# A hybrid decoder trunk on one core: the delta-rule mixer in single steps between half projection units

## The reference

```python
w = -softplus(-(decay_w0 + tanh(wl) @ decay_w2)) - 0.5
decay = exp(-exp(w));  a = sigmoid(aaa_a0 + al @ aaa_w2);  g = sigmoid(gl) @ gate_w2
kk = k * k_k;  kk = kk / max(norm(kk), 1e-12)          # per head of 64
k = k * (1 + (a - 1) * k_a)
# per token, state S (64x64) per head, 8 heads:
S = S * decay + (S @ -kk) (kk * a)^T + v k^T;   y = S @ r
y = groupnorm(y) * gn_g + gn_b + (r * k * r_k).sum() * v;   out = y * g
```

## Time and profile before

| | |
|---|---|
| Median of 3 runs | 1887.74 us (1887.35 to 1894.12) |
| The profiled execution | 1885.17 us, span 1883.4 us |
| Busy: PE, PEld, DVE, ACT, POOL | 1731.8, 1532.1, 1368.5, 1002.6, 31.1 us |
| Mean granted PE clock | 0.969 |
| Read from HBM | 408.09 MB, 218 GB/s over the span |

### The profile page before, as it was taken

One profiled execution on the slowest core, in us unless ns is written; L12 is line 12 of the kernel. 1 busy time (PEld: TensorE's weight loads), 2 busy tenths in 40 slices (PEclk: granted clock), 3 DMA queues, 4 the chain that ended last, 5 costly groups with the idle time before them and its releaser, 6 DMA issues.

```text
span 1883.4 us, 27888 instructions
## 1 busy us (share of the span) xinstructions
PE 1731.8 (92%) x10784; PEld 1532.1 (81%) x10784; DVE 1368.5 (73%) x1242; ACT 1002.6 (53%) x919; POOL 31.1 (2%) x20
## 2 busy tenths in 40 slices
PE   6898998879999789899989599999999999999996
PEld 6797897868999679888888488888888888888885
DVE  5757755675444676766475688989898988888887
ACT  4363243633333344523344376767676776767674
POOL 0000000001000200000000100000000000000000
PEclk9899999998999799999999799999999999999998
DMA  8322322464665343223234598989999999999993
GB/s 262 114 91 90 112 86 91 136 179 134 178 178 178 122 147 112 90 88 93 68 121 168 190 351 321 374 318 379 330 374 331 356 337 360 331 362 354 342 364 121
DMA packets 252061, 411.29 MB, mean 218 GB/s; under 512 B 8400, under 2 KB 133840, under 8 KB 251344
## 3 DMA queue, kind: packets, MB, share of 16 engines
q1 hardware_dynamic: 249440, 400.68, 61.6%
q10 hardware_dynamic: 2544, 9.54, 1.4%
HBM read 408.09 MB, written 2.10 MB: 218 GB/s over the span
## 4 chain that ended last, share of the span: by engine, by line
PE 78%; DVE 14%; ACT 4%; issue 4%; DMA 1%; SPq 0%; DVEq 0%; ACTq 0%
PE W L428 16%; PE W L430 16%; PE W L429 16%; PE Y L428 5%; PE Y L429 5%; PE Y L430 5%; PE Y L596 2%; PE Y L590 2%; PE Y L785 2%; ACT w_hi L952 2%; DVE w_lo L1330 2%; PE W L505 1%; DVE sc L1475 1%; PE Y L505 1%; DVE xt L1492 1%
## 5 line engine op out<-in xcount | busy, mean ns | idle before, releaser
L428 PE MATMUL W<-w_lo,x_hi 128*128 128x512 f32 (+1 forms) x1120 | 393.0, 351 | 9.1 <-DVE x_lo L1629 6.5
L430 PE MATMUL W<-w_hi,x_hi 128*128 128x512 f32 (+1 forms) x1120 | 387.6, 346 | 0.0
L429 PE MATMUL W<-w_hi,x_lo 128*128 128x512 f32 (+1 forms) x1120 | 386.9, 345 | 0.0
L1330 DVE TENSOR_TENSOR w_lo<-raw,w_hi 128x2048 fp32r<-128x2048 f32 x115 | 263.2, 2292 | 165.7 <-ACT w_hi L952 164.6
L1337 DVE TENSOR_TENSOR w_lo<-raw,w_hi 128x2048 fp32r<-128x2048 f32 x144 | 329.7, 2290 | 52.5 <-ACT w_hi L958 52.3
L958 ACT ACTIVATE w_hi<-raw 128x2048 fp32r<-128x2048 f32 x144 | 276.0, 1917 | 83.3 <-PE Y L430 43.7
L428 PE MATMUL W<-x_lo,w_hi 128*128 128x256 f32 x992 | 294.2, 297 | 22.1 <-DVE w_lo L1330 15.7
L1337 DVE TENSOR_TENSOR w_lo<-raw_more,w_hi 128x2048 fp32r<-128x2048 f32 x120 | 275.0, 2291 | 32.0 <-ACT w_hi L958 31.9
L429 PE MATMUL W<-x_hi,w_lo 128*128 128x256 f32 x992 | 285.7, 288 | 0.0
L430 PE MATMUL W<-x_hi,w_hi 128*128 128x256 f32 x992 | 285.4, 288 | 0.0
L958 ACT ACTIVATE w_hi<-raw_more 128x2048 fp32r<-128x2048 f32 x120 | 230.7, 1922 | 67.1 <-PE W L430 43.9
(11 more groups left out here) (278 smaller groups left out, 2097.7 us busy)
## 6 DMA issues: line engine op xcount, KB each, us to landing
raw<-w_in SPq DMA_DIRECT2D x124, 512.0 KB, 4.7
raw<-moe_gate SPq DMA_DIRECT2D x48, 1024.0 KB, 7.0
raw<-moe_up SPq DMA_DIRECT2D x48, 1024.0 KB, 7.7
raw<-moe_down SPq DMA_DIRECT2D x48, 1024.0 KB, 6.2
raw_more<-moe_gate SPq DMA_DIRECT2D x40, 1024.0 KB, 7.5
raw_more<-moe_up SPq DMA_DIRECT2D x40, 1024.0 KB, 7.3
raw_more<-moe_down SPq DMA_DIRECT2D x40, 1024.0 KB, 6.9
raw<-w_branch SPq DMA_DIRECT2D x24, 512.0 KB, 4.4
```

Source lines behind the costliest of these rows:

```text
L428: nc.tensor.matmul(out_ap, lhs[0], rhs[1], start=start, stop=False)
L429: nc.tensor.matmul(out_ap, lhs[1], rhs[0], start=False, stop=False)
L430: return nc.tensor.matmul(out_ap, lhs[0], rhs[0], start=False, stop=stop)
L1330: V.tensor_tensor(w_lo[u % 3][:], raw[u % 3][:], w_hi[u % 3][:].bitcast(F32), ALU.subtract)\
```

## The change

1. Entries ("front", kind, q) and ("back", kind, q) take half a unit each: PE issues 24 matmuls, ACT and DVE do the splits of unit u+2 at the front, ACT copies the bank at the back. Nearly every step of the mixer stands between two halves.
2. Levels 1 to 5 of the inversion act only inside the two 64x64 blocks on a matrix's diagonal. They are kept compactly (128 partitions x 64): mc, ac, xn and xt[:, :, 0]. Each product is two 64x64 matmuls for each of 8 matrices. Both x and its transpose are updated by matmul and addition, so the transposes go. Level 6 is the corner block alone. The masks cm are cut to this form by POOL at the start.
3. The chain is split in cg, cu and cy; its copies move from DVE to ACT.
4. The sums for the two norms are taken by token (4 products with two columns), square root and reciprocal act on 8 numbers for each partition, and 8 matmuls spread them over the channels (spread, scaled).
5. The token shift becomes ACT's copy times mu, and one DVE operation. ksq, decayed, the copy of y and the squares move to ACT; gn_b is added to the bonus on ACT.
6. The last two units of gate1 move ahead of the end of the second inversion.

```diff
+    ("front", "rkv", 5), ("spread", 0), ("kk", 0), ("back", "rkv", 5), ("prep", 0),
+    ("units", "conv", 0, 1), ("decayed", 0), ("shift", 1),
+    ("front", "conv", 1), ("tok", 0), ("bonus", 0), ("back", "conv", 1), ("scores", 0, 0),
+    ("front", "conv", 2), ("scores", 0, 1), ("back", "conv", 2), ("compact", 0), ("lora_w", 1), ("rate_w", 1),
+    ("front", "conv", 3), ("invert", 0), ("back", "conv", 3), ("mx", 0, 1), ("shift", 3),
+    ("front", "conv", 4), ("dx", 0, 1), ("back", "conv", 4), ("mx", 0, 2), ("shift", 5),
+    ("front", "conv", 5), ("dx", 0, 2), ("back", "conv", 5), ("mx", 0, 3), ("decay", 1), ("lora_a", 1), ("rate_a", 1),
+    ("front", "gate0", 0), ("dx", 0, 3), ("back", "gate0", 0), ("mx", 0, 4), ("ksq", 1), ("exps", 1), ("conv", 0),
+    ("front", "gate0", 1), ("dx", 0, 4), ("back", "gate0", 1), ("mx", 0, 5), ("ss", 1), ("knorm", 1),
+    ("front", "gate0", 2), ("dx", 0, 5), ("back", "gate0", 2), ("mx", 0, 6), ("conv", 1), ("osplit", 0), ("spread", 1), ("kk", 1),
...
+    ("units", "qkv", 3, 4), ("compact", 1),
+    ("front", "qkv", 4), ("invert", 1), ("back", "qkv", 4), ("mx", 1, 1), ("rope", 2),
...
+    ("front", "gate1", 3), ("dx", 1, 5), ("back", "gate1", 3), ("mx", 1, 6), ("dx", 1, 6),
+    ("cg", 1, 0), ("cu", 1, 0), ("cy", 1, 0), ("cg", 1, 1), ("cu", 1, 1), ("cy", 1, 1), ("yrow", 1),
+    ("mean", 1), ("var", 1), ("scaled", 1), ("osplit", 1), ("heads",), ("units", "branch1", 0, 2),
...
+            def over_channels(to):
+                for c in range(NT):
+                    for m in range(2):
+                        for h, half in enumerate(HALVES):
+                            last = nc.tensor.matmul(tiles(to[:])[half, m, c * P:(c + 1) * P],
+                                                    inv[:, c, m, h:h + 1].to_broadcast([P, HD]), ident, start=True, stop=True)
...
+            def blocks(bank, left, right):
+                for u in range(8):
+                    for half in HALVES:
+                        last = nc.tensor.matmul(tiles(bank[:], 8)[half, u, :], left(half, u), right(half, u), start=True, stop=True)
...
+            def dx(l, p, v):            # PE
+                if v < TOP:
+                    blocks(Y[1], lambda half, u: mc[half, u, :], lambda half, u: xt[half, u, 0, :])
+                    last = blocks(Y[2], lambda half, u: xt[half, u, 0, :], lambda half, u: mc[half, u, :])
...
+            def front(l, kind, q):      # ACT
+                split_hi(layer_unit(l) + UNIT0[kind] + q + 2)
...
+            def compact(l, p):          # ACT
+                act.wait_ge(sem("score_ready"), 8 * n + 8)
+                for half in HALVES:
+                    last = A(ac[half], sc[half, :, 0, half], ACT.Copy)
...
+            def front(l, kind, q):      # DVE
+                u = layer_unit(l) + UNIT0[kind] + q
+                split_lo(u + 2)
...
+            def invert(l, p):           # DVE
+                dve.wait_ge(sem("ac_ready"), n + 1)
+                link(V.tensor_tensor(mc[:], ac[:], each_of_8(0), ALU.mult))
+                mark(V.tensor_tensor(xt[:, :, 0, :], mc[:], each_of_8(TOP), ALU.add), "xt0_ready", n + 1)
+                mask_level(n, 1)
...
+            def dx(l, p, v):            # DVE
+                V.tensor_tensor(xt[:, :, 0, :], xt[:, :, 0, :], tiles(Y[1][:], 8), ALU.add)
+                mark(V.tensor_tensor(xn[:], xn[:], tiles(Y[2][:], 8), ALU.add), "x_ready", 5 * n + v)
+                if v < TOP - 1:
+                    mask_level(n, v + 1)
```

More of the change, by code:

```diff
@@ L125 @@
     ("units", "rkv", 1, 2), ("shift", 0), ("lora_w", 0), ("rate_w", 0),
[L126 to L148, removed]
@@ L149 @@
-    ("units", "gate1", 1, 2), ("chain", 1, 0), ("chain", 1, 1), ("finish", 1),
-    ("units", "gate1", 2, 4), ("osplit", 1), ("heads",), ("units", "branch1", 0, 2),
+    ("units", "rkv", 2, 3), ("decay", 0), ("lora_a", 0), ("rate_a", 0),
+    ("spill",), ("units", "rkv", 3, 4), ("shift", 2), ("ksq", 0), ("exps", 0),
+    ("units", "rkv", 4, 5), ("ss", 0), ("knorm", 0), ("shift", 4),
+    ("front", "rkv", 5), ("spread", 0), ("kk", 0), ("back", "rkv", 5), ("prep", 0),
+    ("units", "conv", 0, 1), ("decayed", 0), ("shift", 1),
@@ L558, in scores @@
                 pe.wait_ge(sem("bonus_ready"), n + 1)
[L559 to L569, removed]
@@ L631, in chain @@
                     cols = slice(c * P, (c + 1) * P)
-                    pair = [(h, hc, half) for h, mm, hc, half in heads if mm == m]
+                    pair = [(h, hc, half) for h, mm, hc, half in HEADS if mm == m]
                     for h, hc, half in pair:
@@ L904, in _ @@
             handlers = {"units": units, "lora_w": lora_w, "lora_a": lora_a, "ss": ss, "tok": tok, "scores": scores, "invert": invert,
-                        "level": level, "chain": chain, "finish": finish, "rope": rope, "heads": heads, "att_scores": att_scores,
+                        "front": front, "back": back, "mx": mx, "dx": dx, "cg": cg, "cu": cu, "cy": cy, "spread": spread,
+                        "mean": mean, "var": var, "scaled": scaled, "rope": rope, "heads": heads, "att_scores": att_scores,
                         "probs_t": probs_t, "att_out": att_out}
@@ new lines, in ksq @@
+            def ksq(l, p):
+                n = 2 * l + p
+                act.wait_ge(sem("shifted"), 7 * l + order[2 + p] + 1)
+                if n:
+                    act.wait_ge(sem("score_done"), 8 * n)
+                    act.wait_ge(sem("bonus_done"), n)
+                for m in range(2):
+                    last = A(t6[:, m, :], rkvl[:, 4 + 2 * p + m, :], ACT.Copy, scale=par_col(l, "k_k", 2 * p + m))
+                last.then_inc(sem("kscaled"), 1)
+                act.wait_ge(sem("kscaled"), n + 1)
+                A(td[:], t6[:], ACT.Square).then_inc(sem("ksq_ready"), 1)
@@ L1256, in _ @@
             split_hi(1)
-            handlers = {"units": units, "lora_in": lora_in, "rate_w": rate_w, "rate_a": rate_a, "exps": exps,
-                        "knorm": knorm, "tok": tok, "invert": invert, "level": level, "finish": finish,
-                        "heads": heads, "softmax": softmax, "probs_t": probs_t, "att_out": att_out,
+            handlers = {"units": units, "lora_in": lora_in, "rate_w": rate_w, "rate_a": rate_a, "exps": exps, "shift": shift,
+                        "ksq": ksq, "knorm": knorm, "decayed": decayed, "tok": tok, "bonus": bonus, "compact": compact,
+                        "invert": invert, "mx": mx, "cg": cg, "cu": cu, "yrow": yrow, "mean": mean, "var": var,
+                        "front": front, "back": back, "heads": heads, "softmax": softmax, "probs_t": probs_t, "att_out": att_out,
                         "osplit": osplit, "msplit": msplit, "spill": spill_stream}
@@ L1825, in _ @@
             dve.wait_ge(sem("prm_full"), 16)
-            handlers = {"units": units, "shift": shift, "conv": conv, "decay": decay, "ksq": ksq, "kk": kk, "prep": prep,
-                        "decayed": decayed, "bonus": bonus, "scores": scores, "invert": invert, "level": level, "chain": chain,
-                        "finish": finish, "rope": rope, "att_scores": att_scores, "softmax": softmax,
+            link(V.tensor_scalar(rest[:], prm[:, :, PAR["mu"]:PAR["mu"] + 14], -1.0, 1.0, ALU.mult, ALU.add))
+            handlers = {"units": units, "front": front, "back": back, "shift": shift, "conv": conv, "decay": decay, "knorm": knorm,
+                        "kk": kk, "prep": prep, "bonus": bonus, "scores": scores, "invert": invert, "dx": dx, "cy": cy,
+                        "mean": mean, "var": var, "scaled": scaled, "rope": rope, "att_scores": att_scores, "softmax": softmax,
                         "att_out": att_out, "osplit": osplit, "msplit": msplit}
```

422 lines of the change are left out of this document (264 added, 158 removed), and 6 rows, old and new, of the table TIMELINE.

## The result

The changed kernel takes 1895.68 us (median of 14 runs, 1893.55 to 1896.44); the kernel before took 1888.63 in the same comparison. The ratio is 1.0036, with a 95% interval of 1.0025 to 1.0047 (numbers in square brackets behind a ratio are such intervals from here on): 7 us slower, within the 0.5% that I called no change, and outside my range of 1836 to 1893. The forecast was 1862, a gain of 26.

What follows compares the result with a forecast made beforehand. PE bounds the kernel (78% of the chain). Per layer: -22.8 inversion, +3.4 norm spreading, +6.3 waits and slow clock = -13.1, -26 in all; 1885.2 - 26 + 2.6 = 1862 us, range 1836 to 1893.

Steps and rivals of the forecast that it cites:

- Inversion on PE: Both inversion passes on PE: block-product pairs taken at 0.053 us, 11.4 us saved a pass, 22.8 a layer.
- Changing tile shape: Tile-shape changes on PE between units and block products: 0.18 us a step, some 16 of 26 steps, 3 a layer.
- The reserve of 2: Allowance of 2 us among each layer's waits for the inversion's block products.
- Tail: From mx6 of pass 1 to branch1, nothing covers the chain: 26 us, 14 of it PE's own work, wait 12.
- Slow clock: Behind four gaps of over 4 us in each layer's stretch: 2.15 us each, 8.6 together.
- the other sign: Forecast wrong if a layer's stretch, third rkv unit to branch1's first unit, is outside 264 to 292 us; 276 to 277 expected.
- Waits: Walked PE waits: 2.7 at the spread, 6.3 and 4.8 at invert's passes, 5.8 in pass 0's levels; all terms 48.6.
- the 2.1 of scores: PE's waits at scores: 1.9 us in pass 1 for the scaled result, a w_lo split and bonus; 0.2 in pass 0.
- the 1.3 of the corner: Chain of pass 0: the corner waits 1.3 us for conv, osplit and a w_lo split on DVE.
- 1 (waits don't come): The three long waits stay away or are half as long, splits being earlier than walked: 1818 or 1840 us; chance 0.16.
- 2 (no pairing): Inversion's block products do not pair: two halves cost 0.107 us, not 0.053; 28 a layer, 1918 us; chance 0.13.
- 3: No change: added table loads for Square and Identity, longer slow clock after long gaps; 13 a layer, 1888 us; chance 0.19.

Runs made afterwards that it cites:

- run 5: Changed kernel with the eight products of each u step sorted by tile shape instead of alternating: 1881.02 us, ratio 0.9965 to the kernel before.
- run 1: Changed kernel with idle matmuls (results unused) on PE at the tail's hand-overs, from level 6 of pass 1 on: 1881.69 us, ratio 0.9958.
- `combined`: Changed kernel with late w_lo splits, ksq and exps behind the next split, sorted u products and idle matmuls in the tail: 1827.41 us, ratio 0.9669.
- run 7: Kernel before with only part 6: gate1's units 2 and 3 moved ahead of the second chain and group norm: 1911.18 us, ratio 1.0116.
- run 6: Changed kernel with part 6 undone, gate1's units 2 and 3 again behind the chain of pass 1: 1900.65 us, ratio 1.0064.
- `tail_units`: The kernel of run 6: changed kernel with gate1's units 2 and 3 moved back behind the chain of pass 1; 1900.65 us.
- `u_sorted`: The kernel of run 5: changed kernel with the u step's eight products sorted by shape; 1881.02 us.

## Why the prediction was wrong

The waits that I had walked came, nearly at their size, and the inversion got cheaper. Two things on PE failed: the size of small products and of their changes of shape, and the clock, which I priced behind four long waits only and left at full speed in the tail and behind it. By steps, for layer 0:

1. *Inversion on PE, and "Changing tile shape".* The step that failed first is the sizing of small products. I took 0.053 us for a pair of block products by halving the columns of the earlier trace rows; it is 0.065 to 0.067 (the level shown above): (0.22 + 0.30) x 10 levels = 5.2 us. I took 0.18 us for a step's two changes of shape and counted 16 steps, 3 us. A half unit costs 0.19 more than 2.88 between products of narrower shapes and 0.09 more where one neighbour is 128x128. Of the layer's 40 halves some 30 are of the first kind and 10 of the second (an estimate from the order), so 6.6, 3.6 over: I had charged only the steps where PE was the limit. The u step has no term of its own in the prediction; its eight instructions of before, 0.111 apart, are 0.9. Now it has sixteen, alternates two shapes and takes 2.05 (run 5): 2.3 more in pass 0, 2.3 in the tail. The reserve of 2 did not hold this: 5.2 + 3.6 + 2.3 - 2 = 9.1 over.
The Trainium skill (TensorEngine Tiling (Array Packing), Key Properties) says a change of tiling mode drains the engine. The traces agree in that each change costs, and put the price at 0.1 to 0.14 us; I had cited it and then not looked for shapes that alternate inside a step.

2. *"Tail" and "Slow clock".* 26 us were predicted, 36.5 measured. Of the 10.5, 6.8 are slow clock (29.67 in run 1), 1.7 the shapes of u (27.99 in `combined`), and 2 are left for the other small steps. I priced slow clock for four gaps of over 4 us at one unit's 2.15 and made the sum of the tail at full-clock durations. But the earlier trace rows show one long wait ahead of dense work. The tail is a row of waits of 0.5 to 2.4 us between small products, and its granted clock was 0.62. At the lower level PE's steps took 1.6 to 2.2 times as long (a pair of u's instructions 0.40 us for 0.26, the mean 1.87 for 0.86), and the work behind was slow as well: branch1's first unit 2.65 longer, two more units 0.8 and 0.6. That is 4 of the 5.6 us a layer by which time moved outside the stretches. I had ruled this out by making the sum inside them, and had named it as a sign that the forecast is wrong; the other sign, a stretch outside 264 to 292, did not show. The 5.6 is a mean: by the end of attention the two layers stand 5.3 and 5.6 us later against the ends of their stretches, then layer 0 gives 1.7 back and layer 1 loses another 2.6 up to its end, 1.5 of it where the same instructions ran at clock 0.91 instead of 1.00.

3. *Waits.* They came 5.3 us a layer shorter than walked: 2.2, 5.9, 3.4 and 4.6 for 2.7, 6.3, 5.8 and 4.8, 1.6 for the 2.1 of scores, and none that is listed for the 1.3 of the corner. (The 2.7 is itself a slip: its terms give 11.9 less 9.5, 2.4.) This made the miss smaller, not the forecast better. The slow clock behind them (the first unit or half unit and the small products after each, over their full-clock times) came to about 8.1, predicted 8.6.

Together: 9.1 + 10.5 - 5.3 - 0.5 = 13.8 over in the stretch, measured 12.5; the 1.3 between them is not explained. With the 5.6 behind the stretch (the span's 10.2 and the 1.0 that the stretches gained, halved) that is 18 a layer and 36 in all, for the 33.7 by which the median missed.

The rivals: 1 (waits don't come) is refuted by the list of waits. 2 (no pairing) is refuted by 0.067 a pair and by level 6. 3 gave the right time, 1888, for half a right reason: slow clock longer than priced, but no added table load, and its extra clock stood behind long gaps, where the trace has it in the tail (6.8) and behind (4). Part 6 of the change, costed within the tail, costs 11 us a layer alone on the kernel before (run 7), and undoing it on the changed kernel loses 2.5 a layer (run 6), so its price depends on what else stands in the tail.

Open: what of the 14.7 us of run 5 is owed to the sorting itself. 6.7 are changes of shape; the other 8 go with the shorter slow spell, and no run sets the one without the other. How long a slow spell lasts also moves between kernels at places that no edit touches: the half unit behind invert of pass 1 takes 4.05 us in the changed kernel, 4.26 in `tail_units` and 4.98 in `u_sorted`. There is one trace of each kernel, so part of the 8 may be such a shift.

## What to carry to other kernels

Walking every engine's order gave each wait to within a microsecond or two; do it for the clock too: price a serial chain of small steps on PE, without dense work between, with the slow clock in mind, and the unit behind it too. Order small products by tile shape. When an engine idles on a split for a later unit while the critical operand is ready, put the critical one first: three edits of a few lines turned +7 us into -53, and idle matmuls in the bare tail into -61.

## What the runs showed of the hardware

- The granted clock falls also without any long wait. In the tail of the changed kernel it fell twice, at 292.1 and 305.8, with no wait above 0.9 us up to then, and its mean is 0.62; the same steps with idle matmuls in the gaps run at 1.00 and end 6.8 us sooner, although PE then has 88 more instructions to issue.
- Two instructions of 64x64 blocks with 64 columns in opposite quadrants of PE take 0.065 us together; in one quadrant (level 6) a single one takes 0.067, so the two overlap. A pair of 128x64 with 128 columns takes 0.107: half the rows and columns save two fifths, not half.
- Each change of tile shape costs 0.1 to 0.14 us at full clock: 0.19 for the two around a half unit, and 0.84 for six inside a u step.
